# First norm's pieces grouped by input tiles, and spatial units set between token units, in a gMLP and stick-breaking decoder trunk

## The reference, cut to what matters

```python
D_MODEL = 1024; SEQ = 1024; DEPTH = 2; CHUNK = 128
GMLP_WIDTH = 2048; GMLP_GROUPS = 8; N_HEADS = 16; D_FF = 4096

def _gmlp_mixer(h, w_in, v_norm_g, w_s, b_s, w_out):
    uv = jax.nn.gelu(h @ w_in, approximate=False)
    u, v = jnp.split(uv, 2, axis=-1)
    v = _rmsnorm(v, v_norm_g)
    v = v.reshape(B, n_chunks, CHUNK, GMLP_GROUPS, GMLP_WIDTH // GMLP_GROUPS)
    z = jnp.einsum("gts,bnsgc->bntgc", jnp.tril(w_s), v) + b_s.T[None, None, :, :, None]
    return (u * z.reshape(B, S, GMLP_WIDTH)) @ w_out

def reference(x, c, ...):
    for layer in range(DEPTH):
        mod = c @ mod_w[layer] + mod_b[layer]
        sh1, sc1, g1, sh2, sc2, g2 = jnp.split(mod, 6, axis=-1)
        h = _rmsnorm(x, norm_g[layer, 0]) * (1 + sc1) + sh1
        y = _gmlp_mixer(h, ...) if layer == 0 else attention(h, k_shared, v_shared)
        x = x + g1 * y
        h = _rmsnorm(x, norm_g[layer, 1]) * (1 + sc2) + sh2
        x = x + g2 * (jnp.square(jax.nn.relu(h @ w_up)) @ w_down)
        if layer == 0:                       # shared keys and values
            k_shared, v_shared = ...
    return x
```

## Time and profile before

| | us |
|---|---|
| median of 3 runs | 2787.9 |
| lowest, highest | 2787.83, 2791.03 |
| the profiled execution's own time | 2790.93 |
| its span | 2789.2 |
| TensorE busy | 2708.3 (97%) |
| VectorE busy | 1270.2 (46%) |
| ScalarE busy | 769.7 (28%) |
| mean granted TensorE clock | 0.991 of full speed |

### The profile page before, as it was taken

The page is one execution under the profiler, slowest core; times in us unless marked ns, Lnnn a source line. Parts: engine busy times, 40 slices in busy tenths (PEclk is TensorE's granted clock), DMA queues, the critical chain, the costliest instruction groups (busy, mean ns, idle before and its releaser), DMA issues.

```text
span 2789.2 us, 35403 instructions
## 1 busy us (share of the span) xinstructions
PE 2708.3 (97%) x14144; PEld 2282.1 (82%) x14144; DVE 1270.2 (46%) x1480; ACT 769.7 (28%) x1100; POOL 149.4 (5%) x147
## 2 busy tenths in 40 slices
PE   6898999999999999999999998999999999999999
PEld 4898999778888888888889887777788888888887
DVE  4436334446544444443533544888544333333332
ACT  3436222113311211112211334555323121211210
POOL 0000000000000000000000002555200000000000
PEclk9999999999999999999999998999999999999999
DMA  5321322222223233221222364555211111111111
GB/s 227 118 94 61 137 90 90 76 91 69 78 97 105 91 98 96 92 90 46 104 74 80 106 180 124 127 126 127 101 40 48 49 53 45 45 52 46 53 46 68
DMA packets 85339, 246.78 MB, mean 88 GB/s; under 512 B 8064, under 2 KB 32640, under 8 KB 82048
## 3 DMA queue, kind: packets, MB, share of 16 engines
q1 hardware_dynamic: 85248, 245.48, 27.9%
HBM read 216.09 MB, written 29.36 MB: 88 GB/s over the span
## 4 chain that ended last, share of the span: by engine, by line
PE 93%; DVE 4%; ACT 2%; issue 1%; DMA 1%; SPq 0%; ACTq 0%; DVEq 0%
PE PS L1489 22%; PE PS L1491 22%; PE PS L1490 21%; PE PS L1591 5%; PE PS L1592 5%; PE PS L1593 5%; PE PS L1843 4%; PE PS L1831 2%; PE PS L1810 1%; PE PS L1807 1%; PE PS L1763 1%; DVE TN L1001 1%; DVE H_LO L1008 1%; DVE VC_LO L1109 1%; PE PS L1604 0%
## 5 line engine op out<-in xcount | busy, mean ns | idle before, releaser
L1489 PE MATMUL PS<-H_HI,W_HI 128*128 128x512 f32 x1280 | 501.8, 392 | 3.1 <-DVE H_LO L1008 3.1
L1491 PE MATMUL PS<-H_HI,W_LO 128*128 128x512 f32 x1280 | 498.4, 389 | 0.0
L1490 PE MATMUL PS<-H_LO,W_HI 128*128 128x512 f32 x1280 | 498.1, 389 | 0.0
L1166 DVE SCALAR_TENSOR_TENSOR X<-PS,MODV,X 128x1024 f32<-128x1024 f32 x148 | 189.9, 1283 | 471.1 <-PE PS L1491 471.1
L1489 PE MATMUL PS<-HID_HI,W_HI 128*128 128x512 f32 x1024 | 398.9, 390 | 0.0
L1491 PE MATMUL PS<-HID_HI,W_LO 128*128 128x512 f32 x1024 | 398.4, 389 | 0.0
L1490 PE MATMUL PS<-HID_LO,W_HI 128*128 128x512 f32 x1024 | 398.4, 389 | 0.0
L349 ACT ACTIVATE W_HI<-RAW 128x1024 fp32r<-128x1024 f32 x208 | 216.7, 1052 | 623.5 <-PE PS L1491 551.2
L1591 PE MATMUL PS<-W_HI,H_HI 128*128 128x256 f32 x1216 | 350.4, 288 | 18.4 <-ACT V L680 7.0
L1592 PE MATMUL PS<-W_HI,H_LO 128*128 128x256 f32 x1216 | 347.6, 286 | 0.0
L1593 PE MATMUL PS<-W_LO,H_HI 128*128 128x256 f32 x1216 | 347.4, 286 | 0.0
(11 more groups left out here) (151 smaller groups left out, 3218.1 us busy)
## 6 DMA issues: line engine op xcount, KB each, us to landing
RAW<-in_wt SPq DMA_DIRECT2D x208, 512.0 KB, 3.4
MODRAW<-in_modw SPq DMA_DIRECT2D x96, 512.0 KB, 4.3
QK<-qk_scratch SPq DMA_DIRECT2D x16, 768.0 KB, 6.3
MOD<-in_modw SPq DMA_DIRECT2D x8, 1024.0 KB, 18.2
qk_scratch<-KOUTA SPq DMA_DIRECT2D x16, 512.0 KB, 5.4
qk_scratch<-KOUTB SPq DMA_DIRECT2D x16, 512.0 KB, 4.7
QK<-qk_scratch SPq DMA_DIRECT2D x16, 512.0 KB, 8.1
VH<-v_scratch SPq DMA_DIRECT2D x16, 512.0 KB, 7.9
```

The lines of the kernel that those rows point to most:

```text
L1166: dve.scalar_tensor_tensor(X[:, k, :], flat(acc(u % 2)), MODV[:, gate + k:gate + k + 1], X[:, k, :], ALU.mult, ALU.add).then_inc(sem["acc_ ...
L1489: pe.matmul(dst, w_hi, m_hi, start=first, stop=False)
L1490: pe.matmul(dst, w_hi, m_lo, start=False, stop=False)
L1491: return pe.matmul(dst, w_lo, m_hi, start=False, stop=last)
```

## The change

It does three things.

1. The weights' copy `CCR` of `c` has 32 columns, and `mod_rows` uses four column tiles of 32 (partitions 0, 32, 64 and 96 of bank 6), input tile `k` on tile `k % 4`. `SEL` picks four partitions.
2. The pieces of the first norm go by groups of two input tiles, both token halves of a group one after the other (`FIRST_PIECES`). All four weight cuts come ahead of the first piece, on ScalarE ahead of `keep_rows(0)` too. The four pieces of a group follow its `mod_first`.
3. Spatial units use banks 1 and 3 alone and two buffers of cuts. They are set one by one behind token units: units 0 to 6 behind the V units 9 to 15 of `LAST_V`, units 7 to 15 behind the first nine U units. The first two pairs of U tiles (16 units) are written out ahead of a loop that runs three times in place of four. `X` is loaded again four weight tiles later.

```diff
+SPATIAL = [(r, half) for back in range(2) for half in range(2) for r in range(4 * back, 4 * back + 4)]
+FIRST_PIECES = [(half, k) for g in range(4) for half in range(2) for k in (2 * g, 2 * g + 1)]
 # SyncE
+            v_tiles(None, range(T_U, T_U + 4))
             sp.wait_ge(sem["sp_z"], 2 * NCHUNK)
             sp.wait_ge(sem["sp_zd"], 2 * NCHUNK)
             sp.dma_start(X[:], xT).then_inc(sem["x_back"], 16)
 # ScalarE, start
-            keep_rows(0)
-            cut_hi(act, Count(0))
-            cut_hi(act, Count(1))
-            hi_piece(0, 0)
-            ...
+            for n in range(4):
+                cut_hi(act, Count(n))
+            keep_rows(0)
+            for g in range(4):
+                hi_piece(0, 4 * g)
+                hi_piece(0, 4 * g + 1)
+                if g < 3:
+                    keep_rows(g + 1)
+                hi_piece(0, 4 * g + 2)
+                hi_piece(0, 4 * g + 3)
             act.wait_ge(sem["crow_in"], 16)
             ...
 # ScalarE, spatial
+            def sp_cut(s):
+                ...
+                if s >= 2:
+                    act.wait_ge(sem["sp_full"], s - 1)
+                ...
+            def sp_out(s):
+                act.wait_ge(sem["sp_full"], s + 1)
+                act.wait_ge(sem["sp_lo"], s + 1)
+                ...
+                z.then_inc(sem["sp_z"], 1)
             for u, (pair, chunk) in enumerate(LAST_V):
                 ...
-                v_gelu(Count(T_V + 2 * pair), Count(U_SP - 16 + u), chunk, slice(pair, pair + 1))
+                v_gelu(Count(T_V + 2 * pair), Count(U_U - 16 + u), chunk, slice(pair, pair + 1))
+                if u == 8:
+                    v_root(0)
+                if u >= 8:
+                    sp_cut(u - 8)
+                if u >= 10:
+                    sp_out(u - 10)
 ...
+            for u, (pair, chunk) in enumerate(FIRST_U):
+                if u < 8:
+                    sp_cut(8 + u)
+                if u < 10:
+                    sp_out(6 + u)
+                ...
+                u_gelu(Count(U_U + u))
 # VectorE, start: the four cuts, then for each g mod_first(g) and its four pieces
+            for n in range(4):
+                cut_lo(dve, Count(n))
+            for g in range(4):
+                mod_first(g)
+                ...
+                pieces(0, 4 * g, 4 * g + 4)
 # VectorE, spatial: v_gain(u) or u_mul(u), sp_cut and sp_out at the places of ScalarE's
 # TensorE
-                    x = k % 2
-                    mm = pe.matmul(PS[HD * x:HD * x + HD, 6, :], CCR[:, k, :], MOD0[:, g, :, k, :], start=(k < 2),
-                                   stop=(k >= KT - 2))
+                    x = k % 4 * MROWS
+                    mm = pe.matmul(PS[x:x + MROWS, 6, :], CCR[:, k, :], MOD0[:, g, :, k, :], start=(k < 4),
+                                   stop=(k >= 4))
-                pe.wait_ge(sem["h_lo"], k + 1)
+                pe.wait_ge(sem["h_lo"], FIRST_PIECES.index((0, k)) + 1)
+            def spatial_unit(s):
+                half = SPATIAL[s][1]
+                pe.wait_ge(sem["sp_lo"], s + 1)
+                if s:
+                    pe.wait_ge(sem["sp_z"], s)
+                    pe.wait_ge(sem["sp_zd"], s)
+                ...
             for u, (pair, chunk) in enumerate(LAST_V):
                 ...
                 token_unit(Count(T_V + 2 * pair), chunk, u % 2)
+                if u >= 9:
+                    spatial_unit(u - 9)
+            for u, (pair, chunk) in enumerate(FIRST_U):
+                ...
+                token_unit(Count(T_U + 2 * pair), chunk, u % 2)
+                if u < 9:
+                    spatial_unit(7 + u)
```

More of the change, by code:

```diff
@@ L109 @@
 SECOND = [(p, c) for p in range(2) for c in range(4, 8)]
+SPATIAL = [(r, half) for back in range(2) for half in range(2) for r in range(4 * back, 4 * back + 4)]
+FIRST_U = [(p, c) for p in range(2) for c in range(NCHUNK)]
 LAST_V = [(p, c) for half in range(2) for p in range(6, 8) for c in range(4 * half, 4 * half + 4)]
@@ L266, in build @@
         WS_LO = at("WS_LO", [P, GROUPS, CHUNK], F32R, RX + 4 * KB)
-        VC_HI = at("VC_HI", [P, 3, W // 2], F32R, RX + 8 * KB)
-        VC_LO = at("VC_LO", [P, 3, W // 2], F32R, RX + 20 * KB)
+        VC_HI = at("VC_HI", [P, 2, W // 2], F32R, RX + 8 * KB)
+        VC_LO = at("VC_LO", [P, 2, W // 2], F32R, RX + 16 * KB)
         GBC = at("GBC", [P, W], F32, RX + 24 * KB)
@@ L415, in _ @@
             sp.dma_start(X[:], xT).then_inc(sem["x_back"], 16)
-            with sp.Fori(0, 4) as i:
-                v_tiles(i, range(T_U, T_U + 4))
+            with sp.Fori(0, 3) as i:
+                v_tiles(i, range(T_U + 4, T_U + 8))
             def m_tiles(first, stop, ld_mod, i=None, step=0, t_end=TILES):
@@ L630, in hi_piece @@
             def hi_piece(r, i):
-                half, k = divmod(i, 8)
+                half, k = piece_at(r, i)
                 sh = NORMS[r][0] + k
@@ L1654, in _ @@
                         token_unit(n, chunk, u % 2)
+            def spatial_unit(s):
[4 more added lines that the diff above has]
+                    pe.wait_ge(sem["sp_zd"], s)
+                else:
+                    pe.wait_ge(sem["ws_lo"], 1)
+                for g in range(4):
+                    sl = slice(g * 2 * P, (g + 1) * 2 * P)
+                    dst = PS[:, 1 + g // 2 * 2, (g % 2) * 2 * P:(g % 2 + 1) * 2 * P]
+                    mm = three(dst, WS_HI[:, 4 * half + g, :], WS_LO[:, 4 * half + g, :], VC_HI[:, s % 2, sl],
+                               VC_LO[:, s % 2, sl], True, True)
+                mm.then_inc(sem["sp_full"], 1)
@@ L1664, in _ @@
                 if u < 2:
-                    pe.wait_ge(sem["v_gelu"], U_SP + 2)
-                    pe.wait_ge(sem["ws_lo"], 1)
-                else:
-                    pe.wait_ge(sem["sp_z"], u - 1)
-                    pe.wait_ge(sem["sp_zd"], u - 1)
-                for g in range(4):
-                    sl = slice(g * 2 * P, (g + 1) * 2 * P)
-                    dst = PS[:, 2 * (u % 2) + g // 2, (g % 2) * 2 * P:(g % 2 + 1) * 2 * P]
-                    mm = three(dst, WS_HI[:, 4 * half + g, :], WS_LO[:, 4 * half + g, :], VC_HI[:, u % 3, sl],
-                               VC_LO[:, u % 3, sl], True, True)
```

213 lines of the change are left out of this document (96 added, 117 removed).

## The result

| | before | after |
|---|---|---|
| median, us (5 runs each) | 2789.05 | 2804.03 |
| lowest, highest | 2787.83, 2791.03 | 2802.65, 2805.45 |
| profiled execution | 2790.93 | 2803.88 |
| its span | 2789.2 | 2802.1 |
| mean granted clock of TensorE | 0.991 | 0.988 |

The ratio is 1.0054 with a 95% interval from 1.0042 to 1.0065: slower by 15.0 us. The forecast was 2799 with a range from 2790 to 2809, that is 11.2 above the median of three runs of the kernel before (2787.9).

A forecast was written before the change was run, and what follows sets the result against it. TensorE, busy 97% of the span, was taken as the bound, so only its waits counted. Start -18.2, spatial idle +20.4 and clock +9.0 gave +11.2: 2799 us against the median of 2787.9, range 2790 to 2809.

The forecast's parts named there:

- whole start: From kernel start through the first token units: shorter chains, no gelu wait and no clock loss behind it, -18.2 us.
- waits in front of units 1 to 6: Spatial units behind V units: copies queue behind gelu and gain, TensorE idles 4.4 us six times, 26.4.
- in front of unit 0: First spatial unit: a 5.4 us chain through root, cut and low part against one 2.9 token unit, 2.5 idle.
- in front of units 7 to 14: Spatial units among U units: a 3.6 us chain beside a 2.9 token unit, 0.7 idle each, 5.6 in all.
- clock in the V units: Lower clock behind each of the six 4.4 us waits, 1.5 each: +9.0 us, bounds 0 and some 20.
- (a) to (d): Start: mod_rows(0) takes 3.3, VectorE's weight cuts end at 30.2, first unit at 33.6, first token unit at 63.3.
- 7.9 for eight matmuls alone: Start, mod_rows: estimated time without column tiles, used to argue that two abreast halved it to 3.65.
- (e): Clock at the start: 1.5 us saved with the 7.03 wait, start's gain 18.2, weight-cut wait near 105 unchanged.
- four tiles don't run abreast: Rival on mod_rows at the start: tiles of 32 columns bring no gain, +17, 2805 us; chance 0.10.
- the clock stays up: Rival on the V units: no clock loss behind the waits, the two parts cancel, +2, 2790 us; chance 0.12.
- the swinging of the clock through the U units: Rival on the U units: waits of 0.7 hold the lower clock, some 22 more, 2821 us; chance 0.05.
- The copies hide under the token unit: Rival on the spatial units: six waits become 0.7 each, 12.3 idle, no lower clock, -20, 2768 us; chance 0.06.

The follow-up runs named there:

- e6: Changed kernel with the conditioning's rows on two column tiles of 64 in place of four of 32: 2809.39 us, ratio 1.0075 to the kernel before.
- e7: Changed kernel with the gain vector's load issued ahead of the modulation load on SyncE's queue: 2801.98 us, ratio 1.0049 to the kernel before.
- e4: Changed kernel with the spatial copies ahead of the V units' gelu and gain, and ahead of the U units' cuts: 2764.45 us, ratio 0.9913.
- e3b: Changed kernel with 24 useless matmuls into free bank 5 before each spatial unit behind V units 10 to 15: 2796.93 us, ratio 1.0028.
- e2: Kernel before with only the spatial part of the change, its start left as it was: 2819.84 us, ratio 1.0108.
- e3: Changed kernel with the same 24 useless matmuls as e3b, but into bank 6, which holds the conditioning row: 2797.78 us, ratio 1.0030.
- e5: Changed kernel with copies ahead of gelu and gain behind the V units only; U units keep cuts ahead of copies: 2772.87 us, ratio 0.9941.
- e1: Kernel before with only the start of the change, spatial units left as their own stage: 2774.41 us, ratio 0.9949.
- e9: As e4, with the gain vector's load first and each spatial unit one token unit later, cuts left in place: 2776.12 us, ratio 0.9956.

## Why the prediction was right

The forecast's mechanism and both signs held, and the sum came out close: +11.2 forecast, +13.4 found at the first transpose, +12.9 in the profiled spans and +15.0 by the medians. Step by step:

| step | forecast | found | from |
|---|---|---|---|
| `mod_rows` on four tiles | 3.3, 1.8 | 3.64, 1.92 | timeline |
| weight cuts on VectorE end | 30.2 | 30.07 | timeline |
| first unit | 33.6 | 33.64 | timeline |
| first token unit | 63.3 | 62.98 | timeline |
| whole start | -18.2 | -17.4 | 107.69 to 90.32 |
| waits in front of units 1 to 6 | 6 of 4.4 | 6 of 4.25 | waits, timeline |
| in front of unit 0 | 2.5 | 2.54 | timeline |
| in front of units 7 to 14 | 8 of 0.7 | 7 of 0.57 | timeline |
| clock in the V units | +9.0 | +11.3 | below |

(a) to (d) hold. `mod_rows(0)`, behind the long idle of the start, took 3.64 and not 3.3, 1.9 times the later ones: it ran at the lower clock throughout. (The last step of the 6.63 before was at the upper level already, 0.60 long where the others are 1.06, and the end of a length isn't halved.) e6 shows that these rows are on the path. The forecast's 7.9 for eight matmuls alone was too high: it multiplied 1.98 by four, and with it the time in the pipeline that a length has at its end. By start times, one record of such a float32 matmul costs 0.43, so sixteen take 6.9 and some 7.0 with the end. In `mod_rows` the two or four records of one step start together and the steps are again 0.43 apart: eight steps on two tiles (3.65), four on four tiles (1.92). So four tiles abreast lose nothing in a step, and 7.0 against 1.92 is a factor of 3.6 because the end is paid once in either. The Trainium skill ("TensorE: Matmul & The Clock Gate", section "Measured speedup vs the span model") has 2.38 times for three tiles; no such loss is seen in these rows.

In (e) one sentence was wrong: "The wait for the weight cut near 105 stays as it is". It grew from 2.69 to 4.04. VectorE's order was the same, as I had said, but what it waited for was not: the gain vector's load stood behind a load that waits for the conditioning row, and the conditioning row's copy is now the last thing before the token units. I had read VectorE's order and not SyncE's. e7 takes exactly this back. With it, 0.3 at the first token unit and a clock's part of 1.7 in place of 1.5, the start's -18.2 became -17.4.

The copies behind gelu and gain: the six waits are there at 4.25, and e4 shows that the place in the queues makes them, with nothing else changed. By starts, a wait costs 0.22 more than its row says: seven periods of the U units are 5.11, and 36 matmuls at 0.12 are 4.32, so 0.79 for a wait of 0.57. The waits then cost 6 x 4.47 + 2.76 + 7 x 0.79 = 35.1, against 34.5 forecast.

The clock: 6 x 1.5 had about the right price, but too few stretches: there was a seventh behind the wait of 2.54, and one was longer. Periods from unit 0 to unit 6 are 10.31, 10.84, 10.29, 10.28, 10.29 and 10.27, and 4.32 + 4.47 = 8.79 is what the work and the wait take, so 1.5, 2.05 and four times 1.5: 9.5. From unit 6 to 7 it is 6.10 with no wait, 1.8 more. In all 11.3. e3b, with the clock at 1.00, has 8.80.

A small gain that I had not seen: three waits of 0.31 between U units, at 336.99, 383.64 and 430.27 before, are gone, 3 x 0.53 = 1.6. With them the account closes: -17.4 + (35.1 - 14.1) + 11.3 - 1.6 = +13.3, against 13.4 found. In part it was luck that the sum was so near: without this gain of 1.6 it would have been off by 3.7.

Of the rivals, "four tiles don't run abreast" was refuted by 1.92 against 3.65, "the clock stays up" by the windows, and so was the swinging of the clock through the U units: 0.57 us of wait in every 5.11 left it at 1.00. The Trainium skill's section "A second HAM failure mode: psum-queue depth-cycling" (same page) says that short idles between groups of matmuls that cycle through accumulator banks make the clock swing; these units don't show it. In the V units the clock did swing, but the waits there were 4.25 long. "The copies hide under the token unit" was wrong of this kernel, yet right in what it would take. Its 2768 rested on copies that come ahead of the gelu, and e4 is that kernel, at 2764, with less idle than the 12.3 of the rival: the wait of 2.54 and the two of 1.1.

## What to carry to other kernels

When a unit is set between two others on one engine, look at each of the other engines' queues for what stands ahead of the work that releases it: a result that has long been there can wait behind work that isn't there yet. Put the release (here the copy) at the place where its input comes, ahead of anything that waits for later input, and move all queues by the same step. An order that is unchanged on one engine says nothing of its times if another queue feeds it.

## What I had not expected of the hardware

- Waits of one length can bring the clock down or not. The wait of 2.54 us in front of spatial unit 0 was followed by a slow stretch in the changed kernel, e2, e3b and e6, and not in e3, e4, e5 or e7. One of 2.43 was in e1 and not in before. Waits of 1.84 (e5), 2.03 and 2.51 (e9) brought it down. Those of 1.70 and less in e9, one of 1.72 in before and in e1, and six in a row of 1.38 in e3b did not, and all six of 4.25 in the changed kernel did. So in this kernel a wait of 2.4 or 2.5 us has a hidden price of 0 or 1.5 us, and a profile can show either.
- The slow stretch mostly does not lie in the wait but behind it, where TensorE is busy: from 216.9 after a wait that ended at 215.57. Once it began within the next wait (at 223.7, while TensorE waited until 225.88), lasted to 230.5, and cost 2.05 in place of 1.5.
- 144 useless matmuls in six waits made the kernel 7 to 8 us faster. Taking the waits away was worth 39.
